# Sums of the modulation rows by transposes and VectorE, and an adaptive-norm start in two column halves

## The reference, cut to what matters

```
# first block
mod = silu(c) @ w_ada + b_ada                 # 1024 x 3072
shift, scale, gate = split(mod, 3)
h = rms_norm(x, norm_gain) * (1 + scale) + shift
proj = h @ w_in                               # q, k, v, z, ...
...
x = x + gate * (y @ w_out)
# second block, for i in range(2)
mod = silu(c) @ ada_w[i] + ada_b[i]           # 1024 x 6144: sh1, sc1, g1, sh2, sc2, g2
mod_c = silu(c_ctx) @ ada_w[i] + ada_b[i]     # the context's, in layer 0
a = rmsnorm(h, norm1[i]) * (1 + sc1) + sh1
h = h + g1 * mixer(a)
f = rmsnorm(h, norm2[i]) * (1 + sc2) + sh2
h = h + g2 * swiglu(f)
```

## Time and profile before

| what | before |
|---|---|
| three runs, us | 1784.34, 1792.2, 1791.21 |
| median, us | 1791.21 |
| profiled execution, us; its span | 1788.7; 1786.9 |
| TensorE busy | 1720.8 us, 96% |
| VectorE busy | 976.8 us, 55% |
| ScalarE busy | 679.1 us, 38% |
| transfers | 202.02 MB, mean 113 GB/s |

### The profile page before, as it was taken

How to read it: one execution, slowest core, us unless ns; L and a number is a source line. 1 busy time by engine, 2 the same in 40 slices (tenths; PEclk the granted TensorE clock), 3 DMA queues, 4 the chain that set the end, 5 groups by cost and what they waited for, 6 DMA issues and landing times.

```text
span 1786.9 us, 23061 instructions
## 1 busy us (share of the span) xinstructions
PE 1720.8 (96%) x8968; PEld 1411.6 (79%) x8968; DVE 976.8 (55%) x1803; ACT 679.1 (38%) x1417; POOL 61.2 (3%) x119
## 2 busy tenths in 40 slices
PE   4899999999999999899999999999999899999999
PEld 2777777777999999777788887887888788888887
DVE  4666466666866776666555554346555533333232
ACT  3434555554545555554222222223222422222221
POOL 0000000000000000000000000000000000000000
PEclk8899997899999999998999999998999999999999
DMA  8886332212223131221666555432443233333332
GB/s 302 218 244 162 97 92 86 71 37 72 65 60 99 45 99 44 83 61 38 188 187 184 174 175 156 121 109 84 120 125 97 71 95 94 95 94 95 97 110 77
DMA packets 290215, 202.02 MB, mean 113 GB/s; under 512 B 76247, under 2 KB 272072, under 8 KB 289082
## 3 DMA queue, kind: packets, MB, share of 16 engines
q1 hardware_dynamic: 266942, 133.21, 26.5%
q0 software_dynamic: 15536, 56.37, 10.5%
q10 hardware_dynamic: 7628, 10.97, 1.8%
HBM read 197.33 MB, written 5.28 MB: 113 GB/s over the span
## 4 chain that ended last, share of the span: by engine, by line
PE 88%; DVE 6%; ACT 2%; issue 2%; DMA 2%; ACTq 1%; SPq 0%; DVEq 0%
PE PS L858 13%; PE PS L859 13%; PE PS L860 13%; PE PS L841 5%; PE PS L842 4%; PE PS L840 4%; PE PS L1283 3%; PE PS L1285 3%; PE PS L1284 3%; PE PS L1088 3%; PE PS L1333 2%; PE PS L1357 2%; PE PS L1062 2%; PE PS L1070 1%; PE PS L1345 1%
## 5 line engine op out<-in xcount | busy, mean ns | idle before, releaser
L2014 DVE TENSOR_TENSOR WL<-WS,WH 128x512 fp32r<-128x512 f32 x416 | 268.3, 687 | 269.7 <-ACT WH L1506 269.2
L1506 ACT ACTIVATE WH<-WS 128x512 fp32r<-128x512 f32 x416 | 237.7, 621 | 182.5 <-PE PS L842 140.4
L858 PE MATMUL PS<-A3H,WL 128*128 128x512 f32 x672 | 267.3, 398 | 0.0
L859 PE MATMUL PS<-A3L,WH 128*128 128x512 f32 x672 | 266.5, 397 | 0.0
L860 PE MATMUL PS<-A3H,WH 128*128 128x512 f32 x672 | 264.2, 393 | 0.0
L858 PEld LDWEIGHTS PS<-A3H,WL 128*128 128x128 f32 x672 | 126.2, 188 | 33.5 <-issue 2.8
L860 PEld LDWEIGHTS PS<-A3H,WH 128*128 128x128 f32 x672 | 126.2, 188 | 31.0
L859 PEld LDWEIGHTS PS<-A3L,WH 128*128 128x128 f32 x672 | 126.2, 188 | 28.9
L841 PE MATMUL PS<-GL,WH 128*128 128x512 f32 x352 | 139.7, 397 | 0.0
L840 PE MATMUL PS<-GH,WL 128*128 128x512 f32 x352 | 139.0, 395 | 0.4 <-DVE WL L2014 0.4
L842 PE MATMUL PS<-GH,WH 128*128 128x512 f32 x352 | 139.3, 396 | 0.0
(11 more groups left out here) (362 smaller groups left out, 3506.8 us busy)
## 6 DMA issues: line engine op xcount, KB each, us to landing
AW<-in_ada_w POOLq DMA_DIRECT2D x96, 512.0 KB, 4.2
WS<-in_ffn_w_gate_up SPq DMA_DIRECT2D x88, 512.0 KB, 4.2
WS<-in_ffn_w_down SPq DMA_DIRECT2D x32, 512.0 KB, 4.1
WS<-in_sc_w_in SPq DMA_DIRECT2D x24, 512.0 KB, 3.9
AB<-in_w_ada SPq DMA_DIRECT2D x8, 1024.0 KB, 16.0
WS<-in_w_in SPq DMA_DIRECT2D x32, 256.0 KB, 4.3
WS<-in_diff_w_qkv SPq DMA_DIRECT2D x64, 128.0 KB, 2.6
WS<-in_ffn_w_down SPq DMA_DIRECT2D x16, 384.0 KB, 3.4
```

Source lines behind the costliest of these rows:

```text
L858: mm(PS[:, b, :], wl[:, k, :], hi[:, k, 0:S], start=(k == 0), stop=False)
L859: mm(PS[:, b, :], wh[:, k, :], lo[:, k, 0:S], start=False, stop=False)
L1506: f(weights(p)[0][:, k, :], WS[:, p % 2, k, :], ACT.Copy).then_inc(w_hi, 1)
L2014: tt(lo[:, k, :], WS[:, p % 2, k, :], hi[:, k, :].bitcast(F32), ALU.subtract).then_inc(w_lo, 1)
```

## The change

It has three parts.

- The start. w_ada is loaded by GpSimd, in two column halves b of eight pieces of 512 KB (rows of 2 KB, from both shift and scale), once the small rows are there. VectorE adds one half after the other (add_ada(b)), TensorE sums each half when it is ready, and take_ada(b) adds the bias in front of tiles 0 to 3 and 4 to 7 of the layer norm. The copies US go from VectorE to ScalarE, VectorE's small products GN and SM behind the layer norm, ScalarE's splits of the kcvc panels ahead of the root. The two table transfers go from ScalarE's queue to SyncE's, behind the loads of z0.
- The five parts in att. Each becomes two steps (e0 and e0b, and so on): TensorE transposes four blocks of 128x128 of the sums into one bank, VectorE reduces 128x512 to FOLD (128x4), and adds the bias. SMALL_AT, the table of the places in att, gets e0: 0, e0b: 1, e1: 2, e1b: 3, g0: 37, g0b: 38, g1: 41, g1b: 42, h0: 70, h0b: 71 (before e0: 1, e1: 2, g0: 37, g1: 41, h0: 70).
- The nine layer parts of ada5, ada6, ada7a, ada7b and ada7c: eight transposes into two banks, one reduction of 128x1024, the bias. The part ada_gate stays as it was.

```diff
-SUM_BANKS = (3, 4)
+SUM_BANKS = (3, 5)
+FOLD_BANK = 5
...
+def block_of_ada(x, b):
+    return x.rearrange("p (h n) -> p h n", h=2)[:, :, D // 2 * b:D // 2 * (b + 1)]
...
-w_ada = ins["w_ada"][0].rearrange("(k p) n -> k p n", p=P)
-for k in range(KT):
-    sp.dma_start(AB[:, k, :], w_ada[k, :, 0:2 * D]).then_inc(ada_loaded[k], 16)
...
+if j == 0:
+    sp.wait_ge(rows_out, 16)
+    for head, at, n in ((0, 3 * P - 1, 2 * P), (8, P - 1, S)):
+        sp.dma_start(dist_table[head:head + 8, :, 0:n],
+                     bass.AP(dist_rows.tensor, head * 640 + at, [[640, 8], [-1, P], [1, n]]))\
+            .then_inc(dist_out, 16)
...
+w_ada = ins["w_ada"][0].rearrange("(k p) n -> k p n", p=P)
+pool.wait_ge(vec_in, 16 * len(small_rows()))
+for b in range(2):
+    for k in range(KT):
+        pool.dma_start(block_of_ada(AB[:, k, :], b), block_of_ada(w_ada[k, :, 0:2 * D], b))\
+            .then_inc(ada_loaded[4 * b + k // 2], 16)
-pool.wait_ge(small_free, At("ada_a").small(0) + 1)
+pool.wait_ge(ada_added, 2)
...
-def add_context(a, u, n):
+def turn_sums(name, n, sums, half):
-    add_up(a, u, AC[:, :])
-def add_beside(a, u, n, bank):
+    bank = take_small(att, att_small(name))
+    for f in range(4):
+        c = (4 * half + f) * P
+        m = tp(bank[:, f * P:(f + 1) * P], sums[:, c:c + P], IDENT)
+    m.then_inc(small_done, 1)
+def turn_layer_part(a, u, n, bank=FOLD_BANK):
+    if n > 5:
+        pe.wait_ge(part_fold, n + 1)
-        m = mm(PS[:, bank, f:f + 1], AA[:, n % 2, f * P:(f + 1) * P], ONES[:, 0:1], start=True, stop=True)
+        m = tp(FLAT[:, bank * S + f * P:bank * S + (f + 1) * P], AA[:, n % 2, f * P:(f + 1) * P], IDENT)
...
-a = At("ada_a")
-take_small(a, 0)
-for half in range(2):
-    pe.wait_ge(ada_used, 2 * KT - 2 + half)
-    for f in range(KT):
-        m = mm(PS[:, SMALL, KT * half + f:KT * half + f + 1], AA[:, half, f * P:(f + 1) * P], ONES[:, 0:1],
-               start=True, stop=True)
-m.then_inc(small_done, 1)
+for b in range(2):
+    pe.wait_ge(ada_used, KT * (b + 1))
+    for half in range(2):
+        for f in range(4 * b, 4 * b + 4):
+            m = mm(PS[:, 6 - b, KT * half + f:KT * half + f + 1], AA[:, half, f * P:(f + 1) * P], ONES[:, 0:1],
+                   start=True, stop=True)
+    m.then_inc(ada_summed, 1)
...
-if name == "e0":
-    add_part(att, att_small("e0"), 1)
-elif name == "e1":
-    add_context(att, att_small("e1"), 1)
-elif name == "g0":
-    add_part(att, att_small("g0"), 2)
-elif name == "g1":
-    add_context(att, att_small("g1"), 2)
-elif name == "h0":
-    add_part(att, att_small("h0"), 3)
+if name[0] in "egh":
+    n, sums = {"e0": (1, AA[:, 1, :]), "e1": (1, AC), "g0": (2, AA[:, 0, :]), "g1": (2, AC), "h0": (3, AA[:, 1, :])}[name[0:2]]
+    turn_sums(name, n, sums, 1 if name[2:] else 0)
...
-pe.wait_ge(wo_res, 8 + WO2_BANK.index(SUM_BANKS[x]) + 1)
-add_beside(At("ada5"), x, 4 + x, SUM_BANKS[x])
+pe.wait_ge(wo_res, 8 + WO2_BANK.index(SUM_BANKS[x] + 1) + 1)
+turn_layer_part(At("ada5"), x, 4 + x, SUM_BANKS[x])
...
-add_part(At("ada6"), TAKES.index(a.i), 6 + TAKES.index(a.i))
+turn_layer_part(At("ada6"), TAKES.index(a.i), 6 + TAKES.index(a.i))
...
+for k in range(2):
+    act.wait_ge(small_done, a.small(2 + k) + 1)
+    f(US[:, k * 320:(k + 1) * 320], PS[0:16, SMALL, 0:320], ACT.Copy).then_inc(small_free, 1)
...
-act.wait_ge(rows_out, 16)
-for head, at, n in ((0, 3 * P - 1, 2 * P), (8, P - 1, S)):
-    act.dma_start(dist_table[head:head + 8, :, 0:n],
-                  bass.AP(dist_rows.tensor, head * 640 + at, [[640, 8], [-1, P], [1, n]]))\
-        .then_inc(dist_out, 16)
+for j in range(2):
+    split(At("kcvc"), j)
-layer_norm("norm_a", 0, A1H, slice(0, S), M1, first_panels=At("kcvc"))
+layer_norm("norm_a", 0, A1H, slice(0, S), M1)
...
-def add_ada():
-    both = AA[:, :, :].rearrange("p a n -> p (a n)")
+def add_ada(b):
+    sums = AA[:, :, D // 2 * b:D // 2 * (b + 1)]
-        dve.wait_ge(ada_loaded[k], 16)
+        if k % 2 == 0:
+            dve.wait_ge(ada_loaded[4 * b + k // 2], 32)
+        src = block_of_ada(AB[:, k, :], b)
-            m = ts(both, AB[:, k, :], CS[:, k:k + 1], None, ALU.mult)
-            m.then_inc(ada_used, 1)
+            ts(sums, src, CS[:, k:k + 1], None, ALU.mult).then_inc(ada_used, 1)
-            dve.wait_ge(ada_used, 2 * k - 1)
-            for half in range(2):
-                c = slice(D * half, D * (half + 1))
-                stt(both[:, c], AB[:, k, c], CS[:, k:k + 1], both[:, c], ALU.mult, ALU.add)\
-                    .then_inc(ada_used, 1)
+            dve.wait_ge(ada_used, KT * b + k)
+            stt(sums, src, CS[:, k:k + 1], sums, ALU.mult, ALU.add).then_inc(ada_used, 1)
+def take_ada(b):
+    dve.wait_ge(ada_summed, b + 1)
+    tt(view(M1[:, 4 * b:], [8, 2], [1, 4]), view(PS[:, 6 - b, 4 * b:], [8, 2], [1, 4]),
+       view(VT[:, V_BADA + 4 * b:], [8, 2], [1, 4]), ALU.add).then_inc(ada_added, 1)
+    dve.wait_ge(ada_added, b + 1)
+    stt(NS[:, 4 * b:4 * b + 4], M1[:, 8 + 4 * b:12 + 4 * b], 1.0, VT[:, V_NG + 4 * b:V_NG + 4 * b + 4],
+        ALU.add, ALU.mult).then_inc(ada_added if b else ln_scale, 1)
+    if b:
+        dve.wait_ge(ada_added, 3)
+    else:
+        dve.wait_ge(ln_scale, 1)
...
-for k in range(2):
-    dve.wait_ge(small_done, a.small(2 + k) + 1)
-    copy(US[:, k * 320:(k + 1) * 320], PS[0:16, SMALL, 0:320]).then_inc(small_free, 1)
+dve.wait_ge(cs_ready, 1)
+add_ada(0)
+add_ada(1)
+split(At("kcvc"), 0)
+split(At("kcvc"), 1)
+dve.wait_ge(ln_rs, 1)
+for b in range(2):
+    take_ada(b)
+    layer_norm(0, None, H, A1H, A1L, slice(0, S), M1[:, 8:16], M1[:, 0:8], V_NG, 0, tiles=range(4 * b, 4 * b + 4))
+a = At("mods1")
-dve.wait_ge(cs_ready, 1)
-add_ada()
-split(At("kcvc"), 0)
-split(At("kcvc"), 1)
-dve.wait_ge(small_done, At("ada_a").small(0) + 1)
-tt(M1[:, 0:16], PS[:, SMALL, 0:16], VT[:, V_BADA:V_BADA + 16], ALU.add).then_inc(small_free, 1)
-dve.wait_ge(small_free, At("ada_a").small(0) + 1)
-layer_norm(0, 0, H, A1H, A1L, slice(0, S), M1[:, 8:16], M1[:, 0:8], V_NG, 0)
...
+def fold_sums(u, v, dst, read, c):
+    dve.wait_ge(small_done, att.small(u) + 1)
+    dve.tensor_reduce(FOLD[:, c:c + 4], PS[:, SIDE, :].rearrange("p (f k) -> p f k", k=P), AX.X, ALU.add)\
+        .then_inc(small_free, 1)
+    dve.wait_ge(small_free, att.small(u) + 1)
+    m = tt(dst[:, c:c + 4], FOLD[:, c:c + 4], VT[:, V_ADAB + v + c:V_ADAB + v + c + 4], ALU.add)
+    m.then_inc(read if c else part_fold, 1)
-        dve.wait_ge(small_free, att.small(ATT_SMALLS.index("g1")) + 1)
+        dve.wait_ge(part_fold, 4)
...
-def take_layer_part(stage, u, n, bank=None):
-    if bank is None:
-        take_part(At(stage), u, V_ADAB + 8 * (n - 1), M2, 8 * (n - 1), part_read)
-        return
+def take_layer_part(stage, u, n, bank=FOLD_BANK):
-    c = 8 * (n - 1)
-    tt(M2[:, c:c + 8], PS[:, bank, 0:8], VT[:, V_ADAB + c:V_ADAB + c + 8], ALU.add).then_inc(part_read, 1)
+    c, src = 8 * (n - 1), FOLD[:, :]
+    dve.tensor_reduce(src, FLAT[:, bank * S:(bank + 2) * S].rearrange("p (f k) -> p f k", k=P), AX.X,
+                      ALU.add).then_inc(part_fold, 1)
+    dve.wait_ge(part_fold, n + 2)
+    tt(M2[:, c:c + 8], src, VT[:, V_ADAB + c:V_ADAB + c + 8], ALU.add).then_inc(part_read, 1)
...
-take_layer_part("ada7a", 0, 10, SUM_BANKS[1])
+take_layer_part("ada7a", 0, 10)
```

More of the change, by code:

```diff
@@ L51 @@
     ("norm_a", 1, 0, 0, 1, 0),
-    ("ada_a", 1, 0, 0, 1, 0),
+    ("ada_a", 1, 0, 0, 0, 0),
     ("kcvc", 1, 2, 2, 0, 0),
@@ L57 @@
     ("kvq", 1, 6, 6, 6, 5),
-    ("att", 1, 12, 0, 42, 6),
+    ("att", 1, 12, 0, 47, 6),
     ("w_out2", 1, 4, 0, 0, 0),
@@ L238 @@
 SMALL_AT = {f"f{i}": 4 * i + 4 for i in range(8)}
-SMALL_AT.update({"e0": 1, "e1": 2, "y0": 11, "y1": 19, "l0": 22, "t00": 25, "y2": 27, "t01": 29, "w0": 33, "y3": 35, "g0": 37, "g1": 41, "c0": 54, "c1": 63, "c2": 66, "c3": 86})
+SMALL_AT.update({"e0": 0, "e0b": 1, "e1": 2, "e1b": 3, "y0": 11, "y1": 19, "l0": 22, "t00": 25, "y2": 27, "t01": 29, "w0": 33, "y3": 35, "g0": 37, "g0b": 38, "g1": 41, "g1b": 42, "c0": 54, "c1": 63, "c2": 66, "c3": 86})
 for _j in range(1, 4):
@@ L242 @@
     SMALL_AT.update({f"l{_j}": _b - 8, f"t{_j}0": _b - 5, f"t{_j}1": _b - 3, f"w{_j}": _b, f"y{3 + _j}": _b + 3})
-SMALL_AT.update({"h0": 70, "lam": 74, "y7": N_ATT})
+SMALL_AT.update({"h0": 70, "h0b": 71, "lam": 74, "y7": N_ATT})
 ATT_SMALLS = sorted(SMALL_AT, key=lambda name: SMALL_AT[name])
@@ L348, in hybrid_then_diff_conv @@
         EPSC = sb("EPSC", [P, 1])
+        FOLD = sb("FOLD", [P, 8])
         SM = sb("SM", [P, 64])
@@ L469, in hybrid_then_diff_conv @@
         sq_ready, raw_ready, rs_ready, nrm_out = sem("sq_ready"), sem("raw_ready"), sem("rs_ready"), sem("nrm_out")
-        ada_loaded = [sem(f"ada_loaded{k}") for k in range(KT)]
-        ada_used = sem("ada_used")
+        ada_loaded = [sem(f"ada_loaded{i}") for i in range(KT)]
+        ada_used, ada_summed, ada_added = sem("ada_used"), sem("ada_summed"), sem("ada_added")
         part_in = [sem(f"part_in{s}") for s in range(A_SLOTS)]
```

(27 more changed lines are left out.)

## The result

In twenty executions beside each other the changed kernel took 1797.32 us in the median against 1785.82 of before, a ratio of 1.0047 (95% interval 1.0036 to 1.0058). Measured again beside the experiments (e10) it was 1.0031 (1.0016 to 1.0046). Forecast were 1783.9 us and a range up to 1793. The profiled execution took 1797.71 us, 9.0 more than before's.

A forecast was written before the change was run, and what follows sets the result against it. TensorE was taken as the bound, with 88% of the chain. The terms +1.5 - 4.0 - 4 - 3.5 + 0.3 + 2.4 = -7.3 on 1788.7, plus 2.5 to reach the median, gave 1783.9 us, range 1773 to 1793.

The forecast's parts named there:

- start: Up to z1's split: 8.4 us gained by earlier w_ada sums are given back waiting for z1; +1.5 us.
- five parts of att: Attention stage: transposes instead of one-column passes save 0.88 us each on TensorE, less 0.4 for reductions; -4.0 us.
- the clock behind them: Attention stage: half-clock stretches near 189 and 281 us partly return to full clock; -4 us, bounds -8.5 and +1.
- four parts in up0: In up0 between dense matmuls: transposes save 0.88 us each, with VectorE's reductions hidden beside projection matmuls; -3.5 us.
- junction before up0: Before up0's layer norm: VectorE's longer work moves RAW from 828.75 to 829.0; +0.3 us.
- junctions before conv_in and up1: At 1216.98 and 1405.40, RAW starts without idle time and is moved by one 1.22 us reduction each; +2.4 us.
- E: In the start, the end of the w_ada sums: taken as 38, bounds 36.5 to 43; TensorE starts at E + 5.3.
- The order of table and z1: SyncE's queue in the start: the table's 3.1 MB ahead of z1 hold it until E + 27.9, at 65.9.
- third rival: Start: w_ada under two thirds of best rate, E = 45, start +8.5, no clock gain; 1794.9 us, chance 0.08.
- a new dip elsewhere: Attention stage: a half-clock stretch appearing at another place, counted only as the clock term's upper bound of +1 us.
- second rival: Attention stage: the clock gains nothing from transposes, so that term is 0; 1787.9 us, chance 0.18.
- The cover: In up0: projection matmuls hide the 1.22 us reductions; without that cover each would cost 1.4 us.

The follow-up runs named there:

- e10: The changed kernel once more, measured beside the other experiments on one chip, against the kernel before: ratio 1.0031.
- e13: The kernel before with one more, never used tile of 128x8 (32 bytes a partition), against the kernel before: ratio 0.9973.
- e9: The kernel before, unchanged, measured and profiled a second time as a kernel of its own: ratio 0.9998.
- e8: Start of the change alone, w_ada loaded by SyncE behind the kcvc panels, table written in eight pieces behind z0 to z7, against the kernel before: ratio 1.0025.
- e3: Start of the change alone, w_ada loaded by SyncE ahead of the kcvc panels without waiting for the small rows, against the kernel before: ratio 0.9990.
- e1: As a run, not the part of att: the kernel before with the start of the change alone, against the kernel before: ratio 1.0023.
- e2: Start of the change alone, with the two table transfers back on ScalarE's queue, against the kernel before: ratio 0.9995.
- e4: Start of the change alone, with w_ada loaded by SyncE and the table on ScalarE's queue, against the kernel before: ratio 0.9991.
- e7: The nine layer parts alone changed, with VectorE's reductions moved later in its queue, against the kernel before: ratio 0.9953, median 1780.93 us.

## Why the prediction was wrong, point by point

| term | forecast | measured (traces) |
|---|---|---|
| start | +1.5 | +7.4 |
| five parts of att | -4.0 | 0 to +2.5, with the clock |
| the clock behind them | -4 | about 0: -5 at the two places named, +5.5 elsewhere (means) |
| four parts in up0 | -3.5 | -0.6 |
| junction before up0 | +0.3 | not to be told: 20.9 to 23.6 with before's code |
| junctions before conv_in and up1 | +2.4 | +2.5 for RAW; with the clock, +2.7 and +1.4 against e13, +1.0 and +1.1 against e9 |
| place of the tiles | not seen | -3 |

**The step that failed first** is E, the end of the w_ada sums. I put it at 38, between 36.5 and 43; it is 48.3. Against the 37.0 of "nothing lost" these are 11.3 us, in three terms. The fastest load landed at 23.5 (12.9 + 10.6) and not at 16.9 (13.1 + 3.8): 6.6. The other fifteen took 21.8 us, to 45.3, and not 18.8: 2.9, since the 417 GB/s went by the sum of all transfers (415 here) and w_ada had 361 of them. And the adds behind the last landing took 3.0 us and not 1.3: 1.7, since VectorE needs some 20 us for its sixteen products and sums and was behind the loads at the end. The largest term, the first landing, came from the shortest landing on GpSimd's queue, of single loads with little else under way. The trace of before had a nearer row, w_ada's own eight loads of 1 MB, on SyncE's queue and ahead of all other weights:

```profile
DMA to landing us min/median/max: 9.3/16.0/22.1
```

And e8 against e3 shows what the sum had left out: the kcvc panels, which the change puts in front of w_ada. The upper bound was also worked out wrongly: 8.4 MB at two thirds of 417 GB/s are 30.2 us, which gives E = 47.1 and not 43. At 47.1 the start costs 10.6, and without the clock's gain the time is 1797.0, next to the 1797.3 measured.

**The order of table and z1** was forecast rightly: z1 was held, and landed 24.1 us behind E (27.9 forecast). The chain from z1's split over T, z3 and MW to TensorE's wait shifted as a whole, 8.0 us at z1 and 7.4 at z4. So the third rival came true in its place and its size, at the chance of 0.08, but not for its reason: the rate did not fall to under two thirds, the loads began late. That z1 landed at 72.4, near the rival's 72.9, is luck: E was 3.3 later than its 45 and the table 3.8 quicker. The Trainium skill's rule on ring order within a queue (DMA: Bandwidth & Descriptors, Queues, rings and completion order) fits e1 against e2; e4 shows that a queue of its own did not free z1 either.

**The attention stage.** TensorE's saving came to the tenth (4.4 us less busy, at 41.0 us of half clock in both traces), and went into waits. I had looked at VectorE's load (2.7 us as the bound) and not at the bank: four transposes fill all of a bank that was shared by eight columns before. The clock term read the half-clock stretches as made by the one-column passes ahead of them. At the two places that it named this came true: in the means over the traces 9.7 us of half clock are gone there (10 to 40 and 95 to 140), or 4.9 us of time for a forecast of 4, and 3.7 between 140 and 170. What failed is that nothing would take their place: 12.4 us more stand from 170 us on and 2.2 between 40 and 95, and the stage's half-clock time is 38.5 us for 37.3. The prediction had "a new dip elsewhere" only as its bound of +1. So the second rival was right in the size of this term, 0, and not in its way. Whether transposes as such keep the clock is not settled: the row of 339.1, which I read as full of transposes, is a mixture in which 12 of 29 matmuls are transposes.

**Up0.** The saving of 0.91 a part was right and is there in e7. The cover was not: I named the projection matmuls and VectorE's 6% of the chain as what hides the reduction, and that share is an average over the whole span. What decides is the order in VectorE's queue, where two sums of 1.28 and the reduction of 1.22 stand between one low part and the next.

**The junctions** were right in mechanism: RAW starts without idle time behind the reduction, 1.24 us later in the junction before conv_in (from the part's first pass to the first matmul 9.95 us for 8.71) and 1.26 before up1 (8.77 for 7.51). What comes on top of that in the stretch before conv_in is half clock behind the first matmul (5.9 us in after, 2.9 in e13), and it is not the pause's doing: e9, with before's pause of 8.7 us, has 5.4. Each reduction takes 1.22 us, as estimated from the earlier trace rows.

**The sum** was then -7.3 in the forecast and +9.0 in the traces; the range held E up to 43 and the third rival's lower part only. The prediction named the order of the table and z1 as what could make it wrong most, and that was right; the chance of 0.08 stood on E, which it took for nearly known.
